# First norm of a two-block decoder kernel: row factor applied behind the first four weight units

## The reference

```
h    = x * rsqrt(mean(x*x, axis=-1) + 1e-6) * attn_norm_w
proj = h @ w_in                                  # 1024 x 3080
qkv  = silu(causal_conv(proj[:, 0:1536], conv_w))   # 4 taps per column
```

## Time and profile before

| | |
|---|---|
| median of 3 runs | 760.95 us (760.47 to 761.15) |
| profiled execution, its own time from first to last instruction | 760.4 us |
| TensorE busy | 743.2 us, 98% |
| TensorE weight loads | 684.8 us, 90% |
| VectorE, ScalarE, GpSimd busy | 573.7, 399.0, 25.2 us |
| first matmul / first half product / first split unit | 5.12 / 11.14 / 25.85 us |
| DMA | 148.94 MB, mean 196 GB/s |

### The profile page before, as it was taken

The page is one execution under the profiler, slowest core; times in us unless marked ns, Lnnn a source line. Parts: engine busy times, 40 slices in busy tenths (PEclk is TensorE's granted clock), DMA queues, the critical chain, the costliest instruction groups (busy, mean ns, idle before and its releaser), DMA issues.

```text
span 760.4 us, 13296 instructions
## 1 busy us (share of the span) xinstructions
PE 743.2 (98%) x5256; PEld 684.8 (90%) x5256; DVE 573.7 (75%) x966; ACT 399.0 (52%) x673; POOL 25.2 (3%) x31
## 2 busy tenths in 40 slices
PE   7999999999999999999999999999999999999996
PEld 7988999978999999999889887899889999999995
DVE  5758878776767677678797998977858767676776
ACT  5473445664634443344473444666556565555555
POOL 0031000000000000000003000000010000000000
PEclk9999999999999999999999999999999999999999
DMA  7745354553599888889525523456436655565441
GB/s 300 254 151 167 123 175 159 166 171 107 190 382 345 311 281 278 278 289 376 190 68 192 185 84 112 143 190 197 132 116 206 232 173 172 194 210 172 167 139 56
DMA packets 40526, 148.94 MB, mean 196 GB/s; under 512 B 4496, under 2 KB 4624, under 8 KB 40080
## 3 DMA queue, kind: packets, MB, share of 16 engines
q1 hardware_dynamic: 39600, 142.91, 54.4%
q10 hardware_dynamic: 864, 5.18, 1.8%
HBM read 147.02 MB, written 1.05 MB: 195 GB/s over the span
## 4 chain that ended last, share of the span: by engine, by line
PE 77%; DVE 14%; ACT 4%; issue 2%; DMA 1%; POOL 1%; DVEq 0%; SPq 0%; ACTq 0%
PE bank L1059 14%; PE bank L1062 13%; PE bank L1060 13%; PE bank L1116 6%; PE bank L1117 6%; PE bank L1121 6%; PE bank L1093 4%; DVE wlo L1492 4%; PE bank L1107 3%; PE bank L1253 3%; DVE arena L1498 2%; DVE XN L1498 2%; DVE arena L1492 2%; ACT arena L2077 2%; ACT whi L2077 1%
## 5 line engine op out<-in xcount | busy, mean ns | idle before, releaser
L1059 PE MATMUL bank<-hh,whi 128*128 128x256 f32 x1016 | 290.8, 286 | 0.2
L1062 PE MATMUL bank<-hh,wlo 128*128 128x256 f32 x1016 | 287.5, 283 | 0.8 <-DVE wlo L1492 0.8
L1060 PE MATMUL bank<-hl,whi 128*128 128x256 f32 x1016 | 287.3, 283 | 0.0
L1492 DVE TENSOR_TENSOR wlo<-raw,whi 128x1024 fp32r<-128x1024 f32 x204 | 244.6, 1231 | 26.1 <-ACT whi L2077 26.0
L2077 ACT ACTIVATE whi<-raw 128x1024 fp32r<-128x1024 f32 x204 | 204.2, 1047 | 27.1 <-DMA raw<-w_dram 21.4
L1059 PEld LDWEIGHTS bank<-hh,whi 128*128 128x128 f32 x1016 | 194.6, 192 | 4.5 <-issue 2.2
L1060 PEld LDWEIGHTS bank<-hl,whi 128*128 128x128 f32 x1016 | 194.7, 192 | 1.4
L1062 PEld LDWEIGHTS bank<-hh,wlo 128*128 128x128 f32 x1016 | 194.6, 192 | 1.0 <-DVE wlo L1492 1.0
L1498 DVE SCALAR_TENSOR_TENSOR arena<-bank,cols,arena 128x255 f32<-128x255 f32 (+3 forms) x138 | 58.9, 480 | 28.7 <-ACT arena L2077 27.0
L2077 ACT ACTIVATE arena<-bank 128x256 f32<-128x256 f32 (+2 forms) x75 | 31.9, 445 | 85.0 <-PE bank L1062 65.5
L1117 PE MATMUL bank<-whi,fl 128*128 128x512 f32 x176 | 69.0, 392 | 0.0
(11 more groups left out here) (184 smaller groups left out, 896.9 us busy)
## 6 DMA issues: line engine op xcount, KB each, us to landing
raw<-w_dram SPq DMA_DIRECT2D x268, 512.0 KB, 4.7
arena<-rows_dram ACTq DMA_DIRECT2D x1, 1792.0 KB, 8.2
X<-x_dram SPq DMA_DIRECT2D x2, 512.0 KB, 4.6
arena<-rows_dram ACTq DMA_DIRECT2D x1, 1024.0 KB, 11.7
arena<-bias_dram ACTq DMA_DIRECT2D x1, 1024.0 KB, 15.6
out_dram<-X SPq DMA_DIRECT2D x4, 256.0 KB, 2.0
const<-const_dram ACTq DMA_DIRECT2D x1, 640.0 KB, 3.8
arena<-bias_dram ACTq DMA_DIRECT2D x1, 512.0 KB, 4.7
```

Of the source, the lines that this page charges most:

```text
L1059: e.matmul(o, a, hh[:, k, :], start=(k == 0), stop=False)
L1060: e.matmul(o, a, hl[:, k, :], start=False, stop=False)
L1062: ins = e.matmul(o, wlo[:, s, k * 128:k * 128 + 128], hh[:, k, :], start=False, stop=(k == 7))
L1492: return e.tensor_tensor(out, a, b, op)
```

## The change

The turned rows are no longer scaled by the row factor ahead of the first products. The raw rows are transposed and multiplied by the norm's weights (h32); the first four units are multiplied with these; the row factor, brought along the free axis by a matmul of ones with a diagonal matrix (rbc), is applied to their sums on the way out of the bank (row_scale, into cvs in SBUF, which conv(0) and conv(2) then read), and to the rows themselves (norm_rows, into hn) before these are split. ScalarE alone squares both halves. TensorE runs eight matmuls on a tile of ones from the start, without waiting for a DMA, in place of five on the identity. X's first block comes in two DMAs, the eight norm columns in one of their own, and weight units 0 and 1 are issued ahead of X's second block. Semaphore counts are moved to suit.

```diff
+    def raw_halves(tags, name, fs):
+        for b in range(2):
+            for g in range(2):
+                P.fill(f"turn{b}{g}")
+        P.step("turnx", 0)
+        P.step("raw_rows", 0)
...
+        P.step("square", 0)
+        P.step("sums", 0)
+        P.step("half", ids[0], 0, 0)
+        P.step("half", ids[1], 0, 0)
+        P.step("turnx", 1)
+        P.step("raw_rows", 1)
+        P.step("square", 1)
+        P.step("sums", 1)
+        P.step("half", ids[2], 0, 0)
+        P.fill("rbc")
+        P.step("spread_r")
+        P.step("half", ids[3], 0, 0)
+        for t in range(2):
+            for g in range(2):
+                P.step("norm_rows", t, g)
+        for t in range(2):
+            P.high((t, 0), (t, 1))
+            P.low((t, 0), (t, 1))
+        for n in range(4):
+            P.step("half", ids[n], 1, 0)
...
+        P.need(ids[3], lead=2)
...
     P.step("start")
-    for b in range(2):
-        P.step("square", b)
-        P.step("sums", b)
-    P.step("rows", 0, 0)
-    P.step("rows", 1, 1)
-    P.keep(5)
-    P.turn_to(0, None)
-    P.turn_to(1, None)
-    P.scaled((0, 0), (0, 1), (1, 0), (1, 1))
-    for t in range(2):
-        P.high((t, 0), (t, 1))
-        P.low((t, 0), (t, 1))
-    halves(0, ("cv0", "cv2"), "w_in", (0, 1, 2, 3), lambda: None)
+    raw_halves(("cv0", "cv2"), "w_in", (0, 1, 2, 3))
     P.step("split_ba")
-    P.step("conv", 0)
-    P.step("conv", 2)
+    for f in (0, 2):
+        P.step("row_scale", f)
+        P.step("conv", f)
...
+        ones0, diag, rbc = region(11776, 128), region(11904, 2, 128), region(12288, T)
+        cvs = region(17920, 2, 512)
+        hn = XN[:, :, :].rearrange("p a (k t) -> p (a k) t", t=T)
...
             def start():
+                w.wait_ge("ones0", 1)
+                for _ in range(8):
+                    e.matmul(banks[0][:, 0:128], ones0, ones0, start=True, stop=True)
                 w.wait_ge("const", 16)
+
+            def turnx(b):
+                for g in range(2):
+                    p = open_bank(f"turn{b}{g}")
+                    w.wait_ge(*x_ready(b, g))
+                    for n in range(4):
+                        k = 4 * g + n
+                        ins = e.transpose(p[:, n * 128:n * 128 + 128], X[:, b, k * 128:(k + 1) * 128], K("ident"))
+                    filled(ins, f"turn{b}{g}")
+
+            def spread_r():
+                p = open_bank("rbc")
+                for b in range(2):
+                    w.wait_ge("diag", b + 1)
+                    ins = e.matmul(p[:, tok(b)], ones0, diag[:, b, :], start=True, stop=True)
+                filled(ins, "rbc")
...
-            def square(q):
-                w.wait_ge(*x_ready(q, 1))
-                v = X[:, q, 512:1024]
-                e.tensor_tensor_reduce(out=XN[:, q, 512:1024], in0=v, in1=v, scale=1.0 / 1024, scalar=0.0, op0=ALU.mult,
-                                       op1=ALU.add, accum_out=ss_[:, 2 * q + 1:2 * q + 2]).then_inc(sems["sqd"], 1)
+            def start():
+                e.memset(ones0, 1.0).then_inc(sems["ones0"], 1)
+
+            def raw_rows(b):
+                for g in range(2):
+                    name = f"turn{b}{g}"
+                    p = wait_full(name)[:, :].rearrange("p (k c) -> p k c", k=4)
+                    w.wait_ge("coln", 16)
+                    freed(tt(h32[:, 4 * g:4 * g + 4, tok(b)], p, bc(SCALE[0][:, 4 * g:4 * g + 4], 128), ALU.mult), name)
+
+            def spread_r():
+                w.wait_ge("const", 16)
+                for b in range(2):
+                    w.wait_ge("rpow", b + 1)
+                    ts(diag[:, b, :], K("ident"), rq_[:, b:b + 1], ALU.mult).then_inc(sems["diag"], 1)
+
+            def norm_rows(b, g):
+                wait_after("rbc")
+                wait_after(f"turn{b}{g}")
+                o = slice(4 * g, 4 * g + 4)
+                tt(hn[:, o, tok(b)], h32[:, o, tok(b)], rep(rbc[:, tok(b)], 4), ALU.mult).then_inc(sems["hn"], 1)
+
+            def row_scale(f):
+                p = wait_full(f"cv{f}")[:, :].rearrange("p (n t) -> p n t", n=2)
+                wait_after("rbc")
+                o = cvs[:, f // 2, :].rearrange("p (n t) -> p n t", n=2)
+                freed(tt(o, p, rep(rbc, 2), ALU.mult), f"cv{f}")
...
             def conv(f):
-                p = wait_full(f"cv{f}")
+                if f < 4:
+                    w.wait_ge("cols", 16)
+                    wait_after(f"cv{f}")
+                    p = cvs[:, f // 2, :]
+                else:
+                    p = wait_full(f"cv{f}")
...
-                for half in range(1 if q < 2 else 2):
+                for half in range(2):
...
+            def spread_r():
+                p = wait_full("rbc")
+                freed(af(rbc, p[:, 0:T], ACT.Copy), "rbc")
...
             def start():
-                for b in range(2):
-                    e.dma_start(X[:, b, :], x_d[b * 128:(b + 1) * 128, :]).then_inc(sems[f"x{b}"], 16)
-                e.dma_start(cols[:, :], cols_d[:, :]).then_inc(sems["cols"], 16)
-                for i in range(RAW):
+                for half, sem in enumerate(("x0", "x0b")):
+                    c = half_of(half)
+                    e.dma_start(X[:, 0, c], x_d[0:128, c]).then_inc(sems[sem], 16)
+                e.dma_start(cols[:, 0:8], cols_d[:, 0:8]).then_inc(sems["coln"], 16)
+                fetch(0)
+                fetch(1)
+                e.dma_start(X[:, 1, :], x_d[128:256, :]).then_inc(sems["x1"], 16)
+                e.dma_start(cols[:, 8:NCOL], cols_d[:, 8:NCOL]).then_inc(sems["cols"], 16)
+                for i in range(2, RAW):
                     fetch(i)
```

More of the change, by code:

```diff
@@ L316, in halves @@
         P.need(ids[3], lead=2)
+    def raw_halves(tags, name, fs):
[4 more added lines that the diff above has]
+        P.step("raw_rows", 0)
+        ids = []
+        for n, f in enumerate(fs):
+            if n % 2 == 0:
+                P.fill(tags[n // 2], P.main % 2)
+                P.main += 1
+            i = P.unit("n", name, f, lead=3 - n)
+            P.of[i] = (tags[n // 2], n % 2, ("h", 0))
+            ids.append(i)
+        P.step("square", 0)
[18 more added lines that the diff above has]
+            P.step("half", ids[n], 1, 0)
+            if n % 2:
+                P.fills_bank(ids[n], tags[n // 2])
+            else:
+                P.uses(ids[n])
+        P.need(ids[3], lead=2)
     def last_four(norm, tag, name, ks, src, block):
@@ L828 @@
 PAIRS = [(0, 0), (1, 1), (0, 1)]
-SEMS = """x0 x1 const masks cols bias1 rows gtb bias2 out00 out01 out10 out11 sqd root inv modx hi lo_dve lo_pool used ada
+SEMS = """x0 x0b x1 coln ones0 diag hn cvx const masks cols bias1 rows gtb bias2 out00 out01 out10 out11 sqd root inv modx hi lo_dve lo_pool used ada
 pconst sq ssum rpow xnd xna h_hi h_lo xw sc gt wb wbl csilu cva cvd qkv b1m lam gate gate_act dsq rnorm em atri
@@ L987, in x_ready @@
             if q < 2:
-                return f"x{b}", 16
+                return "x0b" if (q, half) == (0, 1) else f"x{b}", 16
             if q in (2, 3):
@@ L997, in squares @@
         def squares(q, half):
-            return q + 1 if q < 2 else 2 * q - 1 + half - 2 * (q >= 8)
+            return 2 * q + 1 + half - 2 * (q >= 8)
         CONVS = [0, 2, 4, 6, 8, 10]
@@ L1036, in turn @@
                     if g == 0:
[L1037 removed]
+                        w.wait_ge("xnd", t - 1)
                     else:
[L1039 removed]
+                        w.wait_ge("xna", t - 1)
                     for n in range(4):
@@ L1464, in _ @@
             does = {
-                "start": start, "turn": turn, "stat": stat, "front": front, "whole": whole, "half": half, "movv": movv, "mov": mov, "four": four, "ba": ba,
+                "start": start, "turnx": turnx, "spread_r": spread_r, "turn": turn, "stat": stat, "front": front, "whole": whole, "half": half, "movv": movv, "mov": mov, "four": four, "ba": ba,
                 "turn_ba": turn_ba, "lam": lam_, "norms": norms, "decay": decay, "kk": kk, "kq": kq, "lev_first": lev_first,
@@ L1507, in prep @@
                         if c == 1:
-                            w.wait_ge(F["turn10"].b, F["turn10"].full)
-                            w.wait_ge(F["turn11"].b, F["turn11"].full)
+                            w.wait_ge("h_hi", P.hi_at[1, 1])
+                            w.wait_ge("h_lo", P.lo_at[1, 1])
                         if c > 1:
@@ L1681, in conv @@
                                   o[:, j + 1:T], ALU.mult, ALU.add)
-                        if j == 2 and n == 1:
+                        if j == 2 and n == 1 and f < 4:
+                            ins.then_inc(sems["cvx"], 1)
+                        elif j == 2 and n == 1:
                             freed(ins, f"cv{f}")
@@ L2044, in _ @@
             does = {
-                "prep": prep, "square": square, "sumsq": sumsq, "sums": sumsq, "root": root, "rows": rows, "tv": tv, "tl": tl, "addx": addx, "addt": addt, "sums2": sums2, "final": final, "gated": gated, "pre": pre,
```

(8 more changed lines are left out.)

28 lines of the change are left out of this document (17 added, 11 removed).

## The result

| | before | changed |
|---|---|---|
| median | 760.99 us (5 runs, 760.47 to 761.15) | 766.37 us (5 runs, 765.61 to 767.02) |
| ratio | | 1.0069 (95%: 1.0058 to 1.008) |
| profiled execution, span | 760.4 | 764.0 (its time: 765.82) |
| TensorE busy | 743.2 | 745.3 |

The changed kernel is slower by 5.4 us; 763.0 was forecast, 765.0 was the upper end. The sign was right, the size was not.

What follows compares the result with a forecast made beforehand. It took TensorE, busy 98% of the span, as the bound. 2.5 us gained early became 2.1 lost through VectorE's queue: 760.95 + 2.1 = 763.0 us, range 760.2 to 765.0.

Steps and rivals of the forecast that it cites:

- T: TensorE's end of two half products and block 1's transposes, forecast at 11.7 us, other bounds 11.0 and 12.1.
- the wait ahead of unit 6: TensorE, third split unit: issues two matmuls, then waits 3.3 us for the low part behind conv(2) on VectorE.
- POOL's spread: At 49.94 us before, behind conv(6)'s serial chain: it moves later by 2.1 us, and TensorE with it.
- The mask's term: POOL's mask on the bias moves into conv(0) on VectorE: about 0.4 us, bounds 0 and 1.07.
- The step that failed first: Side banks: one fill more shifts their rotation, and later waits by ±0.5 us; costed at nothing.
- The second: Base of the sum: profiled execution spans 760.4 us, its own time; the runs' median 760.95 is 0.55 above.
- rival (c): Clock falls in TensorE's wait before unit 6, costing some 3.1 us more: 764.9 us; chance 0.08.
- (a): Gained and kept: VectorE's low parts of units 6 to 8 don't lag, 2.5 us stay: 758.5; chance 0.13.
- (b): Even: T at 11.0, mask free, slack of 0.5 in the chain: 761.4 to 762.4 us; chance 0.27.
- (d): Early start earns nothing: clock level changes at 11.4 as before, T at 13.7: 765.0 us; chance 0.04.
- X's two loads: X's split issue at the start, one more issue of 0.4 us on SP: costed at nothing.

Runs made afterwards that it cites:

- no_norm_rows: rbc_bank with the four scalings of the normed rows cut to one element each (output not the reference's): 762.57 us.
- reordered: rbc_bank with VectorE's and ScalarE's steps in another order, no work removed: 762.35 us, ratio 1.0014.
- raw_whole_order: raw_whole with reordered's order, and unit 11's modulation row and low part put behind conv(6) on VectorE: 760.41 us, ratio 0.9991.
- rbc_bank: The changed kernel with the spread row's bank fixed by hand (bank 2), taking no turn of the side banks: 765.54 us.
- before_turned: The kernel before with only the rotation of side banks moved on by one bank: 762.47 us, ratio 1.0014.
- changed_again: The changed kernel as it is, run again in the third round: 766.85 us, ratio 1.0072.
- six_sems: The kernel before with six more semaphores, which nothing uses: 761.29 us, ratio 1.0002.
- busy_wait: rbc_bank with eleven idle matmuls put in TensorE's queue ahead of unit 6: 764.88 us.
- raw_whole: rbc_bank with X's first block in one load: 764.41 us.
- early_whole_2: The kernel before with the early start, X's first block in one load, run a second time: 760.56 us, ratio 0.9994.
- early_only: The kernel before with the early start alone, X's first block in two loads: 762.85 us, ratio 1.0017.

## Why the prediction was wrong

**Right, by its own steps.** The start at 1.04 (1.05 forecast), the end of the half products at 23.4 (23.3), the third half product at 11.8 (T = 11.7), row_scale ending at 22.9 (23.15), the taps of conv(2) ending at 31.4 (31.5), the wait ahead of unit 6 in two parts, 0.5 and 2.4 (3.3), conv(6) at 40.6 (40.7), POOL's spread 2.0 later (2.1). The last two owe something to luck: 0.3 of conv(6)'s place is the wait for sums that the fallen clock made late. At the start two errors cancelled: the level changed 2.6 us sooner than I took, and weight unit 0 came 0.7 later than the 6.5 I gave it, so that the first half product began at 7.23 instead of 7.0. no_norm_rows and reordered show that VectorE's queue is the cause.

The mask's term was 0.4 as forecast: conv(0) took 3.09 with POOL's mask at 23.50 beside it, and 2.70 in no_norm_rows, where the mask ran at 21.18, ahead of it. But that was luck. Only 0.6 of the mask's 1.07 us lay on VectorE's work, since the mask had begun before conv(0); the slope that I used, 1.5 in 3.94, gives 0.2 for that. In reordered and raw_whole_order, where VectorE was busy when the mask came, conv(0) took 3.38: the whole mask costs 0.7.

The Trainium skill ("SBUF — State Buffer", Who interferes with whom) has VectorE with two SBUF operands shut out for the whole of such a POOL instruction. The two closer views above agree with it as far as they go, since both taps end 0.28 us behind the mask; the full 1.07, which the prediction allowed by this rule, did not show in any run.

**The step that failed first** was "One fill more shifts the rotation of the side banks, and later waits by ±0.5." It costs 1.3 in the profiled executions (the step near 115 us, which rbc_bank takes away and before_turned alone brings), and 1.0 (before_turned) to 1.3 (rbc_bank against changed_again, two chips) in the medians. The 0.3 near 168 us, which has no term in the sum, is not the rotation's and stays open. I had put the rotation down without looking which later fill would get which bank; that can be worked out from the list.

**The second** was "The profiled execution spans 760.4, its own time; the median of the runs is 760.95, 0.55 above." Time is span + 1.8, so the median execution of the kernel before spans 759.2, and the one that I had taken every row from is 1.2 longer: its level of 1.2 GHz lasted to 11.4, in the profiled executions of kernels with the same start to 8.2 (before_turned) or 9.5 (six_sems). Each us of that costs half a us at the front, in the kernel before: from 60 to 112 us before_turned is 1.6 ahead of it, six_sems 1.0. In the changed kernel a rise that comes somewhat later should cost nothing (no run tries it), since TensorE stands 1.5 us for weight unit 0 in any case; a fall in that wait does cost, as busy_wait and reordered show. So 2.0 against the profiled execution is 3.2 against the median.

**The third** is rival (c), which I kept apart with 0.08, as if it were an exception. In the profiled executions the level fell in the wait at unit 6 in all four in which that wait was whole and the level had not fallen before (the changed kernel twice, rbc_bank, raw_whole). The low level lasted 3.4 or 6.8 us, where I had taken 6.3. Where it lasted 3.4 us, VectorE's lag covered it but for 0.3 to 0.5 (conv(6) waited for TensorE's sums); where it lasted 6.8, the span grew by 1.7. It didn't fall in every execution: one of changed_again and one of raw_whole have a mean granted clock of 0.999. The median of the changed kernel lies 0.6 above its profiled execution (765.82). Its longest two, 766.73 and 767.02, have the lowest mean granted clocks of the five, 0.993 and 0.994, so I put the 0.6 down to the clock; no run isolates it.
Together: 2.0 (0.3 of it the clock's) + 1.3 for the rotation + 0.3 open + 1.2 + 0.6 = 5.4.

**Rivals.** (a) was wrong for the reason given. (b) fell with it. (d) was wrong: the level changed at 4.7. Even so the early start was undone in part by X's two loads, which I had costed at nothing. With them the next 512 KB load was in at 6.7 to 7.9 us, without them at 6.0 to 6.3, and in some executions the level fell ahead of the first half product.

## What to carry to other kernels

Work moved off the front of the bound engine lands on some other engine's queue: write out that queue, in order, up to the next thing the bound engine needs from it, and fill its waits first. Here the same work cost 4 us in one order (raw_whole) and, within the spread, nothing in another (raw_whole_order against early_whole_2). Before adding the sum to a median, ask which kind of execution the profile is, and where a planner hands out buffers in turn, give a new one a fixed place or work out who gets what behind it.

## What the hardware showed that I had not expected

- The granted clock fell in waits of TensorE of 2.4 us (changed kernel at 32.04, with another of 0.5 and two matmuls ahead of it; reordered at 7.5), 2.5 (busy_wait at 7.5) and 3.3 (early_only), but not in waits of 1.2 (early_whole_2, rbc_bank), 1.4 and 1.6 (no_norm_rows) or 1.5 (the changed kernel ahead of 7.2). It read 0.50 for 3.4 or for 6.8 us. The same kernel shows both lengths.
- One load of 512 KB cut into two of 256 KB with rows of 2 KB: the second half is in at 4.3 to 4.8 us, the whole was in at 4.5 to 4.9. The next load of 512 KB lands at 6.7 to 7.9 us instead of 6.0 to 6.3; 0.5 of that is its later issue. The mechanism was not tried.
- A POOL operation that takes 1.07 us beside an idle VectorE stretched one VectorE operation with two SBUF operands from 0.48 to 1.17 us, and took 1.26 to 1.30 itself, when VectorE was busy as it came. Where it came 0.5 us before VectorE's operation, that took 0.87, and POOL's still 1.07.
